# Splitting the operands of the input projection and of the memory keys and values

## The chip, the core and the metric

The kernel runs on one core of a Trainium2 chip. The metric is the device time of one execution in microseconds. Three runs of the kernel before gave 1869.04, 1870.06 and 1871.63 us, median 1870.06.

## The reference

Two layers work on 256 tokens of width 1024. Each layer does, in float32:

- RMSNorm of the residual, then one input projection (1024 rows, seven blocks of up to 256 columns). Its columns feed a state-space mixer (16 groups, 64 complex states each), six latent-attention heads, and six sparse-attention heads with a compressed, a selected and a window branch. The results are normalised and go through an output projection.
- Cross-attention: queries from the residual, keys and values from 256 normalised memory tokens (`kv = rmsnorm(mem, g_mem) @ wkv`), four heads of width 256, an output projection.
- A SwiGLU mixer, dense (width 2816) in layer 0, top-2 of 8 experts (width 3584) in layer 1.

A final RMSNorm gives the output.

## The kernel before

All weights of products with the residual or the memory are packed into chunks of 128 x 2048 float32 (1 MB). SyncE loads them in order into a ring of six slots; the slot of chunk c is loaded again with chunk c + 6 when TensorE has signalled on `weights_used` that it is done with c. A layer has 27 common chunks and then those of its SwiGLU: chunks 0 to 6 are the input projection (tiles `u`, `zA`, `zB`, `q0`, `q1`, `ck` with `cv`, `vs`), 7 to 10 the memory keys (`mk0` to `mk3`), 11 to 14 the memory values (`mv0`, `mv1`, two chunks each), 15 to 18 the output projection `wo`, 19 to 22 the queries of the cross-attention `xq`, 23 to 26 its output `xw`.

There are two kinds of product. The plain one is a float32 matmul, which stands in the trace as two matmul records. The split one takes each operand as an upper and a lower half of type fp32r and sums three matmuls, upper x upper, upper x lower and lower x upper (`split_product`, L398). For that a weight chunk is prepared: ScalarE copies it with rounding into an upper slot (`layer_chunk_upper`, L404), VectorE subtracts the upper half from the chunk in place in the ring (`layer_chunk_lower`, L411). An upper slot is free when the product of chunk c - 2 is done. Before the change chunks 0 to 14 use the plain product and 15 to 26, and all of the SwiGLU, the split one. The token side of `xq` is split by `transposes_upper` on ScalarE (L1499) and `transposes_lower` on VectorE (L1965).

TensorE's order of work is written out by hand. Its results go to PSUM tiles that rotate over five banks (`JOBS`, `ROT`): a tile's matmuls wait until the tile five places earlier was drained by ScalarE or VectorE. Every engine runs its own instruction list in order; semaphores join them.

The order in a layer, by lines of TensorE: transposes of the normalised rows (L1122), the seven projection chunks (L1132 in `features_out`, L1215 to L1243), small products of the latent and compressed attention (L1252 to L1323), then the loop over 18 heads (L1372). An iteration i of it issues the scores of head i + 3, in four iterations (2, 6, 10, 14) a memory-key chunk, in every odd one up to 15 the state input `bu` of one of eight state groups (L1355), the transposes of the probabilities of head i (L1382), the output product of head i - 1 (L1340), and in odd iterations from 3 on the output of the state group before (`state_outputs`, L1362).

A state group passes over three engines: VectorE rotates and scans it (`states`, L1892), GpSimd rotates it back with four operations (L2108 to L2116), TensorE multiplies it (L1365). VectorE also masks the scores (`masked_scores`) and, in iterations 6 and 12 and after the loop, scales the outputs of six heads (`group_outputs`). ScalarE takes the exponentials and drains the transposed probabilities.

After the loop come the memory values (`tokens_out`, L1136), between them the gate of the state-space mixer, then the split part: `wo`, `xq`, cross-attention, `xw`, SwiGLU.

GpSimd builds the rotation table of the states (`ftab`, L2081 to L2101) with the buffer of the memory keys as its scratch, and after the projection scales the transposed memory tokens into `memT`, which lies in `col` (L2105).

Of the kernel before, what the change touches and what calls it, by code (L numbers as in the profile page):

```python
# [91 lines left out]
for _i in range(4):  # L92
    _job(f"hT{_i}", "act")
# [5 lines left out]
for _n, _e in (("cqT", "act"), ("ckvT", "act"), ("hid", "dve"), ("qn0", "act"), ("qr0", "dve"), ("qn1", "act"),  # L99
# [6 lines left out]
SPLIT_FIRST = 15  # L106
# [46 lines left out]
def trunk(nc, x, mem, weights, lparams, consts, onehot, relb, fgain, out, scratch, routed, expert_out):  # L153
    with ExitStack() as ctx:
# [42 lines left out]
        kcT = sb("kcT", [P, 16])  # L197
        pcs = sb("pcs", [96, T])
# [15 lines left out]
        colr = over("colr", [P, KD, T], "col")  # L214
        xor = over("xor", [P, KD, T], "big", KD * T)
# [33 lines left out]
        memT = col  # L249
# [41 lines left out]
        s_out = sem("s_out")  # L291

# [20 lines left out]
        memT_ready = lsem("memT_ready")  # L313
# [33 lines left out]
        moe = []  # L347
        for i in range(2):
            moe.append({n: sem(f"moe{i}_{n}") for n in (
                "onehot", "gathered", "xe", "oh_t", "oh", "silu", "hid", "htr", "ht", "y", "scat", "added",  # L350
                "upper", "split", "ht_up", "xe_up", "index", "sent", "rows0", "rows1", "stored", "ye_free", "fetched",
                "merged")})
# [50 lines left out]

        def layer_chunk_upper(act, l, c):  # L404

            act.wait_ge(landed[c % RING], 16 * (LAYER_CHUNKS // RING * l + c // RING + 1))
            if c >= SPLIT_FIRST + 2:
                act.wait_ge(weights_used, l * LAYER_CHUNKS + RING + c - 1)
            act.activation(upper[:, c % 2, :], ring[:, c % RING, :], ACT.Copy).then_inc(wt_upper[l], 1)  # L409

        def layer_chunk_lower(dve, l, c):  # L411
            dve.wait_ge(wt_upper[l], c - SPLIT_FIRST + 1)
            dve.tensor_tensor(lower[:, c % RING, :], ring[:, c % RING, :], f32(upper[:, c % 2, :]), ALU.subtract).then_inc(wt_split[l], 1)  # L413
# [136 lines left out]
        def moe_pe(pe, m, used, first):  # L550


            def operands(c, count):

                pe.wait_ge(m["split"], count)
# [12 lines left out]
            def turn(i, g):  # L568
                pe.wait_ge(m["hid"], g + 1)
# [4 lines left out]
            def down(i, g, start=False, stop=False, final=False):  # L574
                up, lo = operands(3 * i + 2 if final else 3 * i + 4, 3 * g + (3 if final else 5))
                pe.wait_ge(m["ht"], g + 1)
# [8 lines left out]
            def gather_first():  # L585

                pe.wait_ge(m["onehot"], 1)
# [6 lines left out]
            def turn_rows(e, buf, loads):  # L594

                pe.wait_ge(m[f"rows{buf}"], 16 * loads)
                pe.wait_ge(m["xe"], e)
# [4 lines left out]
            def turn_onehot():  # L602
                pe.wait_ge(m["onehot"], 2)
# [4 lines left out]
            def scatter_last():  # L608
                pe.wait_ge(m["y"], NE + 1)
# [1730 lines left out]
```

## Time and profile before

| What | Value |
|---|---|
| Median of three runs | 1870.06 us |
| The profiled execution itself | 1872.84 us |
| Its span, first to last instruction | 1871.0 us |
| TensorE busy | 1738.9 us, 93% |
| VectorE busy | 1258.9 us, 67% |
| ScalarE busy | 1024.1 us, 55% |
| GpSimd busy | 189.3 us, 10% |
| Chain that ended last: TensorE, VectorE, ScalarE | 84%, 7%, 3% |
| Mean granted TensorE clock | 0.964 |

Busy time is summed over the whole span, in which stages differ. The chain follows the work back from the last instruction: a line in it had nothing slack behind it. The profiled execution took 1.84 us more than its span. The positions below are microseconds from the start of the span; layer 0 covers 26 to 539, layer 1 the rest.

### The profile page before, as it was taken

What the parts mean: (1) busy time and instruction counts of PE and PEld (TensorE: products, weight loads), DVE (VectorE), ACT (ScalarE), POOL (GpSimd) and SP (SyncE); (2) the same over time, 40 slices, a digit from 0 to 9 for tenths busy, and PEclk for the clock granted to TensorE, in tenths of its full rate; (3) what the DMA queues carried; (4) which work ended last, traced back from release to release, by engine and by line L of the source; (5) the groups of instructions that cost most, each with busy time, mean ns of one, the idle gap of its engine ahead of it and who ended that gap; (6) DMA issues with size and microseconds to landing.
All of it is one profiled execution on the core that took longest, in us unless ns stands there. A gap on an engine that the chain in (4) does not pass through costs nothing.

```text
span 1871.0 us, 23430 instructions
## 1 busy us (share of the span) xinstructions
PE 1738.9 (93%) x8104; PEld 1417.6 (76%) x8104; DVE 1258.9 (67%) x1453; ACT 1024.1 (55%) x1156; POOL 189.3 (10%) x248
## 2 busy tenths in 40 slices
PE   6989889799979899896999999999999999999995
PEld 4877477688868675775788888888888888888784
DVE  3245445545442454454799999898999988989895
ACT  2142333443421423342677777777777777777773
POOL 2614100000026141002100000000000000000200
PEclk9989999899989899897999999999999999999998
DMA  8301332755534012322999999999999999999992
GB/s 335 138 23 46 111 117 106 287 197 184 183 120 147 23 46 102 123 98 80 384 373 371 380 384 376 378 371 384 374 382 374 376 386 373 373 379 363 404 382 96
DMA packets 68404, 473.78 MB, mean 253 GB/s; under 512 B 7511, under 2 KB 9047, under 8 KB 13944
## 3 DMA queue, kind: packets, MB, share of 16 engines
q1 hardware_dynamic: 63816, 453.01, 63.7%
q0 software_dynamic: 4528, 19.98, 2.7%
q8 instruction: 36, 0.59, 0.1%
q14 instruction: 24, 0.20, 0.0%
HBM read 460.77 MB, written 12.19 MB: 253 GB/s over the span
## 4 chain that ended last, share of the span: by engine, by line
PE 84%; DVE 7%; ACT 3%; issue 2%; POOL 2%; DMA 1%; DVEq 0%; POOLq 0%; ACTq 0%; SPq 0%
PE bank L400 21%; PE bank L402 21%; PE bank L401 21%; PE bank L1132 5%; PE bank L1145 3%; ACT upper L428 1%; PE bank L571 1%; DVE xel L901 1%; POOL lp L2065 1%; PE bank L1424 1%; PE bank L1215 1%; PE bank L1243 1%; PE bank L1236 1%; DVE xor L1970 1%; DVE lp L1687 1%
## 5 line engine op out<-in xcount | busy, mean ns | idle before, releaser
L434 DVE TENSOR_TENSOR lower<-ring,upper 128x2048 fp32r<-128x2048 f32 x369 | 845.2, 2291 | 145.4 <-ACT upper L428 130.3
L428 ACT ACTIVATE upper<-ring 128x2048 fp32r<-128x2048 f32 x369 | 705.9, 1914 | 115.7 <-PE bank L402 109.6
L400 PE MATMUL bank<-upper,xeu 128*128 128x512 f32 x896 | 360.5, 402 | 5.9 <-DVE xel L901 3.4
L402 PE MATMUL bank<-upper,xel 128*128 128x512 f32 x896 | 351.1, 392 | 0.0
L401 PE MATMUL bank<-lower,xeu 128*128 128x512 f32 x896 | 350.1, 391 | 0.0
L400 PE MATMUL bank<-upper,htu 128*128 128x512 f32 x536 | 209.8, 391 | 5.5 <-DVE htl L915 3.9
L402 PE MATMUL bank<-upper,htl 128*128 128x512 f32 x536 | 208.8, 389 | 0.0
L401 PE MATMUL bank<-lower,htu 128*128 128x512 f32 x536 | 208.7, 389 | 0.0
L400 PEld LDWEIGHTS bank<-upper,xeu 128*128 128x128 f32 x896 | 168.6, 188 | 38.3 <-DVE xel L901 3.6
L402 PEld LDWEIGHTS bank<-upper,xel 128*128 128x128 f32 x896 | 168.5, 188 | 36.1
L401 PEld LDWEIGHTS bank<-lower,xeu 128*128 128x128 f32 x896 | 169.1, 189 | 31.9
L400 PEld LDWEIGHTS bank<-upper,htu 128*128 128x128 f32 x536 | 100.6, 188 | 31.3 <-issue 9.9
L402 PEld LDWEIGHTS bank<-upper,htl 128*128 128x128 f32 x536 | 100.6, 188 | 21.1
L401 PEld LDWEIGHTS bank<-lower,htu 128*128 128x128 f32 x536 | 100.6, 188 | 20.5
L413 DVE TENSOR_TENSOR lower<-ring,upper 128x2048 fp32r<-128x2048 f32 x24 | 54.8, 2291 | 80.6 <-ACT upper L409 80.6
L1132 PE MATMUL bank<-col,ring 128*128 128x256 f32 x448 | 104.4, 394 | 1.9 <-ACT col L1496 1.9
L1132 PEld LDWEIGHTS bank<-col,ring 128*128 128x128 f32 x448 | 89.0, 199 | 15.9 <-ACT col L1496 2.7
L730 ACT ACTIVATE htu<-bank 128x256 fp32r<-128x256 f32 x112 | 43.2, 386 | 99.2 <-PE bank L571 98.9
L726 ACT ACTIVATE big<-bank 128x256 f32<-128x256 f32 x112 | 43.0, 384 | 69.2 <-PE bank L402 69.2
L409 ACT ACTIVATE upper<-ring 128x2048 fp32r<-128x2048 f32 x24 | 45.6, 1908 | 57.0 <-PE bank L402 57.0
L400 PE MATMUL bank<-upper,colu 128*128 128x512 f32 x176 | 70.3, 400 | 5.4 <-DVE coll L824 5.4
L2065 POOL TENSOR_TENSOR small<-small,cst 128x2 f32<-128x2 f32 (+2 forms) x12 | 10.8, 900 | 622.8 <-DVE small L1693 614.9
(354 smaller groups left out, 2256.3 us busy)
## 6 DMA issues: line engine op xcount, KB each, us to landing
ring<-in_weights SPq DMA_DIRECT2D x423, 1024.0 KB, 6.8
routed_rows<-g POOLq DMA_DIRECT2D x1, 4096.0 KB, 27.2
lp<-in_lparams POOLq DMA_DIRECT2D x1, 3634.5 KB, 13.0
lp<-in_lparams SPq DMA_DIRECT2D x1, 3584.0 KB, 26.7
memraw<-routed_rows POOLq DMA_DIRECT2D x7, 512.0 KB, 8.4
expert_rows<-xk POOLq DMA_DIRECT2D x7, 512.0 KB, 8.7
skewed_bias<-big SPq DMA_DIRECT2D x1, 1152.0 KB, 12.3
row<-in_mem SPq DMA_DIRECT2D x1, 1024.0 KB, 4.9
```

The lines of the kernel that those rows point to most:

```text
L400: pe.matmul(to, x_up, w_up, start=start, stop=False, skip_group_check=True)
L401: pe.matmul(to, x_up, w_lo, start=False, stop=False, skip_group_check=True)
L402: return pe.matmul(to, x_lo, w_up, start=False, stop=stop, skip_group_check=True)
L409: act.activation(upper[:, c % 2, :], ring[:, c % RING, :], ACT.Copy).then_inc(wt_upper[l], 1)
L413: dve.tensor_tensor(lower[:, c % RING, :], ring[:, c % RING, :], f32(upper[:, c % 2, :]), ALU.subtract).then_inc(wt_split[l], 1)
L428: act.activation(upper[:, q % 3, :], ring[:, q % RING, :], ACT.Copy).then_inc(done, 1)
L434: dve.tensor_tensor(lower[:, q % RING, :], ring[:, q % RING, :], f32(upper[:, q % 3, :]), ALU.subtract).then_inc(done, 1)
L726: act.activation(gs[:, i % 2, 0, :], banks[i % 2][:, 0:256], ACT.Silu).then_inc(m["silu"], 1)
L730: act.activation(htu[:, i % 2, 0:256], banks[2][:, 0:256], ACT.Copy).then_inc(m["ht_up"], 1)
L1132: ins = mm(b[:, m * T:(m + 1) * T], w[:, k * 256 + m * P:k * 256 + (m + 1) * P], col[:, k, :], start=(k == 0), stop=(k == KD - 1))
L1145: ins = mm(bank(name)[:, :], src[:, 4 * part + k, t * P:(t + 1) * P], w[:, k * 512:(k + 1) * 512], start=(part == 0 and k == 0), stop=(par ...
L2065: return pool.tensor_tensor(out, a, b, op)
```

## The change

Chunks 0 to 14 use the split product too. Nothing of what is computed changes; a float32 product becomes three fp32r products.

- Weight chunks 0 to 14 are prepared by `layer_chunk_upper` and `layer_chunk_lower`. The upper halves of chunks 0 to 10 go by turns to `upper[:, 0, :]` (even, over the first 2048 columns of `attn`) and to the buffer of the memory values (odd, `coluf`); from chunk 11 on to the two slots in `attn` as before. In the loop over heads they are placed where the queries and keys in `attn` are no longer read: the upper half of chunk 7 ahead of the loop, 8 at the end of iteration 3, 9 and 10 after the drain of `mk1` and `mk2`, 11 at the end of iteration 14, 12 at the end of iteration 16. VectorE takes the lower half of chunk 7 ahead of the loop and those of 8, 9, 10, 11 and 12 in iterations 4, 8, 12, 15 and 17.
- The normalised rows are split when drained (upper half in `colr`, lower half in `coll` over the memory keys). TensorE starts `u` and `xq0` block by block as the blocks are drained.
- The window keys in `zB` are computed as tokens x columns and turned by two transposes (`kwT`).
- GpSimd's table uses `g` and the key part of `attn` as scratch; ScalarE waits for the table before it writes keys there. GpSimd scales the memory in place before `vs` is done, and then splits it with four copies and four subtractions.
- The memory is kept in HBM (one DMA out at the start) and read back (one DMA in after layer 0).
- The experts' two passes share their semaphores (counts offset by the pass); the first pass waits on the same counts as before.

```diff
+        def upper_slot(c):
+            if c < MEM_VALUES:
+                return coluf if c % 2 else upper[:, 0, :]
+            return upper[:, c % 2, :]
...
-            if c >= SPLIT_FIRST + 2:
+            if c >= 2:
                 act.wait_ge(weights_used, l * LAYER_CHUNKS + RING + c - 1)
-            act.activation(upper[:, c % 2, :], ring[:, c % RING, :], ACT.Copy).then_inc(wt_upper[l], 1)
+            act.activation(upper_slot(c), ring[:, c % RING, :], ACT.Copy).then_inc(wt_upper[l], 1)
...
+            def features_out(name, c, x_up, x_lo, stage=None):
                 up, lo = split_chunk(c)
...
+                        if stage and m == 0 and k % 2 == 0:
+                            wait_drained(pe, l, f"{stage}T{k // 2}")
...
-                drain_transposes(l, "h", C_MIX)
+                transposes_upper(l, "h", C_MIX)
+                for c in range(2):
+                    layer_chunk_upper(act, l, c)
...
+                act.wait_ge(ftab_ready[l], 1)
                 drained(A(kT[64:96, :, :], bank("ckvT")[64:96, 256:512] ...
...
+                    if i in MEMK and MEMK[i] >= 1 and MEMK[i] + 1 < XH:
+                        layer_chunk_upper(act, l, MEM_FIRST + MEMK[i] + 1)
                     wait_tile(act, l, f"pT{i}")
...
+                    if i + LEAD == NH:
+                        layer_chunk_upper(act, l, MEM_FIRST + 1)
+                    if i + LEAD == HEADS - 1:
+                        layer_chunk_upper(act, l, MEM_VALUES)
+                    if i == HEADS - 2:
+                        layer_chunk_upper(act, l, MEM_VALUES + 1)
...
+                LOWERS = {4: MEM_FIRST + 1, 8: MEM_FIRST + 2, 12: MEM_FIRST + 3, 15: MEM_VALUES, 17: MEM_VALUES + 1}
                 for i in range(LEAD):
                     masked_scores(i)
+                layer_chunk_lower(dve, l, MEM_FIRST)
                 for i in range(HEADS):
                     if i + LEAD < HEADS:
                         masked_scores(i + LEAD)
+                    if i in LOWERS:
+                        layer_chunk_lower(dve, l, LOWERS[i])
                     if i in STATES:
                         states(STATES[i])
...
+                layer_chunk_lower(dve, l, MEM_VALUES + 3)
+                layer_chunk_lower(dve, l, 15)
```

## Rows read from the trace of the kernel before

**Rows 1.** Chain that ended last, in order of time: start us, us, what.
```profile
33.17 9.56 PE bank L1132 x32
42.74 6.91 PE bank L1215 x32
49.65 3.56 PE bank L1223 x32
53.20 3.47 PE bank L1226 x16
56.67 13.81 PE bank L1132 x64
70.49 6.91 PE bank L1236 x32
```

**Rows 2.** Timeline of ScalarE, `wo` and `xq`: start, us, instruction [idle before <-releaser].
```profile
245.74 1.92 ACT L409 ACTIVATE upper<-ring 128x2048 fp32r<-128x2048 f32 x1 [3.53 <-PE bank L402]
251.18 1.92 ACT L409 ACTIVATE upper<-ring 128x2048 fp32r<-128x2048 f32 x1 [3.52 <-PE bank L402]
...
279.24 0.60 ACT L1626 ACTIVATE big<-bank 128x512 f32<-128x512 f32 x1 [3.37 <-PE bank L402]
...
285.00 0.60 ACT L1626 ACTIVATE big<-bank 128x512 f32<-128x512 f32 x1 [3.37 <-PE bank L402]
```

**Rows 3.** Timeline of VectorE in `xq`.
```profile
262.53 3.37 DVE L1970 SCALAR_TENSOR_TENSOR xor<-bank,lp,colr 128x256 fp32r<-128x256 f32 x8 [0.28 <-ACT colr L1505]
...
281.67 2.29 DVE L413 TENSOR_TENSOR lower<-ring,upper 128x2048 fp32r<-128x2048 f32 x1 [3.47 <-ACT upper L409]
```

**Rows 4.** Chain that ended last, after the projection.
```profile
84.30 0.11 PE bank L1252
```

**Rows 5.** Timeline of GpSimd: the table's end, state groups 1 and 2.
```profile
75.64 4.67 POOL L2065 TENSOR_TENSOR big<-big,xk 128x1024 f32<-128x1024 f32 x2
...
136.06 2.50 POOL L2065 TENSOR_TENSOR lp<-g,big 128x512 f32<-128x512 f32 x2 [7.10 <-DVE g L1908]
138.64 1.59 POOL L2065 TENSOR_TENSOR g<-lp 128x256 f32<-128x256 f32 x2
...
144.48 1.41 POOL L2065 TENSOR_TENSOR g<-lp 128x256 f32<-128x256 f32 x2
```

**Rows 6.** Timeline of TensorE in the loop over heads.
```profile
122.96 7.07 PE L1132 MATMUL bank<-col,ring 128*128 128x256 f32 x32
...
140.34 0.62 PE L1365 MATMUL bank<-g,cp 128*32 128x256 f32 x2 [1.55 <-POOLq L2116]
...
177.94 0.41 PE L1351 MATMUL bank<-vs,pt 128*128 128x64 f32 x2 [1.53 <-DVE lp L1687]
...
197.17 0.62 PE L1365 MATMUL bank<-g,cp 128*32 128x256 f32 x2 [2.96 <-POOLq L2116]
```

**Rows 7.** Timeline of VectorE in the loop over heads.
```profile
133.91 0.76 DVE L1687 TENSOR_TENSOR g<-lp 128x256 f32<-128x256 f32 x2
...
139.21 1.31 DVE L1687 TENSOR_TENSOR g<-lp 128x256 f32<-128x256 f32 x2
...
189.44 1.29 DVE L1687 TENSOR_TENSOR lp<-bank,big 128x512 f32<-128x512 f32 x2 [6.04 <-PE bank L1359]
```

**Rows 8.** Timeline of ScalarE, last exponential of the loop over heads.
```profile
188.82 0.50 ACT L1584 ACTIVATE attn<-attn,small 128x256 f32<-128x256 f32 x1
```

**Rows 9.** Chain that ended last: memory values of layer 0, `mk3` of layer 1.
```profile
198.22 15.63 PE bank L1145 x32
...
216.02 13.75 PE bank L1145 x32
...
695.33 7.71 PE bank L1132 x32
```

**Rows 10.** Stages by window: us, busy of PE, PEld, DVE, ACT, POOL; PEclk; DMA share, GB/s.
```profile
198.10:206.00 7.90, 7.90 (x16) 3.39 (x16) 5.15 (x4) 4.23 (x3) 0.00 (x0) 0.78 0.00 0
```

**Rows 11.** Timeline of VectorE behind the loop: the end of the mixer's norms.
```profile
220.68 0.24 DVE L1693 TENSOR_SCALAR small<-small 128x2 f32<-128x2 f32 x2
```

More of the change, by code:

```diff
@@ L98 @@
 _job("vs", "dve", 6)
-for _n, _e in (("cqT", "act"), ("ckvT", "act"), ("hid", "dve"), ("qn0", "act"), ("qr0", "dve"), ("qn1", "act"),
+for _n, _e in (("cqT", "act"), ("ckvT", "act"), ("kwT", "act"), ("hid", "dve"), ("qn0", "act"), ("qr0", "dve"), ("qn1", "act"),
                ("qr1", "dve"), ("kn0", "act"), ("kn1", "act"), ("kn2", "act"), ("vm0", "act"), ("vm1", "act"),
@@ L344, in trunk @@
         flag_ready = sem("flag_ready")
[L347 to L352, printed above, removed]
+        moe_sems = {n: sem(f"moe_{n}") for n in MOE_COUNTS}
+        moe = [ExpertPass(moe_sems, i) for i in range(2)]
         flag_again = sem("flag_again")
@@ L553, in operands @@
             def operands(c, count):
-                pe.wait_ge(m["split"], count)
+                pe.wait_ge(m["split"], m.at("split", count))
                 return upper[:, (first + c) % 3, :], lower[:, (first + c) % RING, :]
@@ L1207, in _ @@
                 transpose_rows("h")
-                wait_drained(pe, l, "hT3")
-                features_out("u", l, 0)
-                w = chunk(l, 1)
-                wait_free(pe, l, "zA")
-                for t in range(TT):
-                    for k in range(KD):
-                        ins = mm(bank("zA")[:, t * 256:(t + 1) * 256], col[:, k, t * P:(t + 1) * P], w[:, k * 256:(k + 1) * 256],
-                                 start=(k == 0), stop=(k == KD - 1))
-                finish("zA", ins)
@@ L1219, in _ @@
-                w = chunk(l, 2)
-                wait_free(pe, l, "zB")
-                for t in range(TT):
-                    for k in range(KD):
-                        mm(bank("zB")[:, t * 114:(t + 1) * 114], col[:, k, t * P:(t + 1) * P], w[:, k * 256:k * 256 + 114],
-                           start=(k == 0), stop=(k == KD - 1))
-                for k in range(KD):
-                    ins = mm(bank("zB")[:, 228:484], w[:, k * 256 + 114:k * 256 + 242], col[:, k, :],
-                             start=(k == 0), stop=(k == KD - 1))
@@ L1228, in _ @@
-                finish("zB", ins)
-                features_out("q0", l, 3)
-                features_out("q1", l, 4)
-                w = chunk(l, 5)
-                for v, name in enumerate(("ck", "cv")):
-                    wait_free(pe, l, name)
-                    for k in range(KD):
-                        ins = mm(bank(name)[:, 0:T], w[:, k * 256 + v * P:k * 256 + (v + 1) * P], col[:, k, :],
-                                 start=(k == 0), stop=(k == KD - 1))
-                    finish(name, ins)
@@ L1239, in _ @@
-                w = chunk(l, 6)
-                wait_free(pe, l, "vs")
-                for t in range(TT):
-                    for k in range(KD):
-                        ins = mm(bank("vs")[:, t * 256:(t + 1) * 256], col[:, k, t * P:(t + 1) * P], w[:, k * 256:(k + 1) * 256],
-                                 start=(k == 0), stop=(k == KD - 1))
-                finish("vs", ins)
+                features_out("u", 0, colr, coll, "h")
+                narrow_tokens_out("zA", 1, colr, coll)
+                narrow_tokens_out("zB", 2, colr, coll)
@@ L1261, in _ @@
                 finish("ckvT", ins)
+                wait_drained(pe, l, "zB")
+                wait_free(pe, l, "kwT")
+                for t in range(TT):
+                    ins = pe.transpose(bank("kwT")[:, t * P:(t + 1) * P], kwr[:, t, :], ident)
+                finish("kwT", ins)
                 wait_drained(pe, l, "ck")
@@ L1693, in mean_eps, with transposes_lower @@
                 return dve.tensor_scalar(ss[:, a:a + n], ss[:, a:a + n], 1.0 / width, EPS, ALU.mult, ALU.add)
+            def transposes_lower(stage, to, gain, n):
+                for i in range(4):
+                    dve.wait_ge(tr_upper[l], n + i + 1)
+                    for k in range(2):
+                        kk = 2 * i + k
+                        ins = dve.scalar_tensor_tensor(to[:, kk, :], bank(f"{stage}T{i}")[:, k * T:(k + 1) * T],
+                                                       cols[:, gain + kk:gain + kk + 1], f32(colr[:, kk, :]),
+                                                       ALU.mult, ALU.subtract)
+                    drained(ins)
             def norm_h(junk, l):
```

252 lines of the change are left out of this document (146 added, 106 removed).

## The prediction

> **What bounds the kernel now.** I read the page first (TensorE busy 93% and 84% of the chain that ended last), then the chain in order of time for layer 0, then the timelines of every engine over 26 to 300 us, where all changed work of a layer lies. The reader is to see three things. In the projection TensorE runs without a gap from 33.17 to 84.3 us, so what a product takes is what the stage takes [rows 1, 4]. In the loop over heads TensorE is not alone: four times it stands and waits, twice 1.55 us (one row stands for both, groups 1 and 3) and once 2.96 us for GpSimd's part of a state group, once 1.53 us for VectorE's `group_outputs(1)` [rows 6]. Any delay of VectorE or GpSimd there is paid in full. After the loop it is TensorE's work again, 15.63 and 13.75 us for the memory values [rows 9]. Both layers have this pattern; I count one and double. The SwiGLU parts are untouched but for semaphore counts that are equal in the first pass; the two new DMAs of 1 MB lie beside work that does not wait for them. Both at nothing.
>
> **What a product takes.** A plain chunk of 256-wide matmuls takes 6.91 us [rows 1]. A split chunk of the same shape is 48 matmuls; in `xq` the drains follow each other in 5.76 us (285.00 - 279.24) [rows 2]. So -1.15 us a chunk, if its halves are there. In 512-wide shape a plain pair takes 13.75 us [rows 9], a split chunk 5.44 us (251.18 - 245.74), a pair 10.88 [rows 2]: -2.87 us. Preparing a chunk costs 1.92 us on ScalarE and 2.29 us on VectorE, some 4.4 us in series with the handover [rows 2, 3].
>
> **Projection, per layer.** Gains: `zA`, `q0`, `q1`, `ck`/`cv`, `vs` five times 1.15 = 5.75; `zB` is 3.56 + 3.47 = 7.03 against 5.76, 1.27 [rows 1]. Costs: `u` may not start before chunk 0 is split. ScalarE comes to it only after draining the rows, when `u` now starts (33.17), so the start moves by about 1.9 + 2.3 = 4.1 us net of the 0.2 us of handover. `u` takes 9.56 against the warm 6.91, so it runs about 5.3 us at half clock [rows 1]; 5.3 us of that leave 25 of 48 matmuls, then 2.8 us: about 8, -1.5. Two transposes at 0.11 each [rows 4]: +0.2. After chunk 0 a slot's refill needs 4.4 us and has 5.76, slack 1.3. That slack hides the preparation, unless GpSimd holds VectorE (below); for the last chunks I add 0.3. The table, which ends at 80.3 [rows 5], ends later: its last part follows the drain of `zB`, which ends where it did (37.3 + 8 + 2 x 5.76 = 56.8, now 56.67) but is drained behind an upper half of 1.9 us, and two subtractions (4.6 us) fall into it: about 87. ScalarE now waits for it, and behind it are the drains of `ckvT`, `kwT` and `qn`; TensorE has the compressed-key product in between, the second `qn` is the first that needs a bank of these: +0.2, bounds 0 and 1.5. The memory split on GpSimd takes 16 operations of at most the 1.25 us of its 512-wide ones [rows 5], so it ends by 107; TensorE asks for it ahead of the loop, `mk0` itself starts at 122.96 and will at 119 [rows 6]: nothing, with some 8 us of cover, and a microsecond per microsecond beyond. Sum: -5.75 - 1.27 + 4.1 - 1.5 + 0.2 + 0.3 + 0.2 = -3.7. Bounds -6 (`u` at full clock) and 0 (each chunk stalls 0.5 us).
>
> **Loop over heads, per layer.** Gain 4 x 1.15 = -4.6. Costs, in order:
> - Chunk 7's subtraction ahead of the loop delays VectorE by 2.3 us; `mk0` follows at once and hides it. If not: 2.3.
> - Iterations 4 and 8: VectorE, having finished state group 1 (3), masks one head and issues the subtraction just while GpSimd works on that group, for which TensorE already waits 1.55 us. What happens if both engines read SBUF shows in a small case: two VectorE operations take 0.76 us, and 1.31 when the second rotation of GpSimd is running; GpSimd's two take 1.59 instead of 1.41 [rows 5, 7]. They take turns and do not overlap: 139.21 starts inside GpSimd's first operation, waits for its end, and GpSimd's next waits for VectorE. With a subtraction of 2.29 us GpSimd's remaining operations wait all of it: +2.25 each, 4.5. Bounds: 0 (no exclusion) and 3.4 each (VectorE's group behind it late as well).
> - Iteration 12: the subtraction stands ahead of `group_outputs(1)`, for which TensorE already waits 1.53 us: +2.25, and about 0.7 for the port: 2.9. Bounds 2.3 and 4.5.
> - Iteration 15: state group 7 waits behind chunk 11's subtraction, and that for its upper half, which ScalarE does after the last exponential (ends 189.3) [rows 8]: 189.3 + 1.9 + 2.3 = 193.5 and 0.1 for the handover, in place of 189.44 [rows 7]: +4.2. TensorE already waits 2.96 us for this group [rows 6]. Bounds 2.3 (if the product of `mk3` ends much earlier) and 5.0.
> - Iteration 17: chunk 12's subtraction comes directly behind the scan of group 7, ahead of GpSimd's first operation by a handover: +2.25. Bounds 0 and 2.3.
> - Drains held up by an upper half (1.9 us of ScalarE) in iterations 3, 6, 10, 14, 16: TensorE has the scores of a later head in between: +0.3.
>
> Sum: -4.6 + 4.5 + 2.9 + 4.2 + 2.25 + 0.3 = +9.55. The four waits become some 3.9, 3.9, 5 and 8 us long. Now the wait of 2.96 us is followed by a granted clock of 0.78 over 7.9 us, that is 3.4 us at 1.2 GHz, and `mv0` takes 15.63 in place of 13.75 us, 1.88 more; in layer 1 `mk3` takes 7.71, 0.80 more, behind the shorter wait [rows 9, 10]. After three of the new waits stands `mk1`, `mk2` or `mk3`. I charge 1.0 each, +3.0; bounds 0 and 1.9 each, and nearer the lower rows, since a drop can fall on a wait. `mv0` has its drop already.
>
> The Trainium skill, "SBUF — State Buffer", section "Who interferes with whom", says that a VectorE instruction with two SBUF inputs contends with a GpSimd instruction that reads SBUF, and that whichever starts first makes the other block fully. The rows agree (0.55 and 0.18 us longer). By this rule the loop is as above; if the two shared the port instead, the loop would be shorter by up to 7.5 us a layer, which is the first rival.
>
> **Memory values to `xq`, per layer.** `mv0` 15.63 to 10.88 + 1.9 = 12.8: -2.85. `mv1`: -2.87, but VectorE subtracts its second chunk only behind the norms of the mixer, which end at 220.9, 4.9 us after `mv1` starts [rows 9, 11]; 4.9 + 2.3 = 7.2 against the 5.44 us that its first chunk gives: 1.8 us of wait, so -1.05. GpSimd's root behind that subtraction, and chunk 15's upper half (1.9 us) ahead of the drain of `mv1`, half of it hidden: +0.9. Sum -3.0; bounds -5 and -1. `xq0` may start when the first of four drained blocks is there instead of all; the eight subtractions take 3.37 us [rows 3], three quarters of it: -2.5; bounds -2.5 and -1 (a colder start).
>
> **Sum.** Per layer -3.7 + 9.55 + 3.0 - 3.0 - 2.5 = +3.35; two layers +6.7. The profiled execution took 1872.84, so 1879.5; the median of the runs lies 2.8 lower: 1876.8.
>
> **Rivals.**
> 1. The ports do not exclude, or VectorE gets its turn where GpSimd has slack, and the clock does not drop. Then iterations 4, 8 and 17 cost nothing, 12 costs 2.3 and 15 4.2: loop +2.2, layer -7.0, time 1870.1 - 14.0 = 1856.1. For it: 51 us of TensorE-bound projection, and the waits before are short. Against: the 1.31 us row. It decides where a subtraction beside GpSimd costs its group under about 0.4 us instead of 2.25. Chance 0.24.
> 2. The waits are there but the clock stays: 1870.1 + 2 x 0.35 = 1870.8. For it: two waits of 1.55 us now have full-speed products behind them. Against: rows 9 and 10. Chance 0.16.
> 3. The projection becomes bound by its preparation: GpSimd holds VectorE in every chunk past the slack of 1.3 us, 0.7 us for six chunks, and all bounds of the loop are high: layer +3.35 + 4.2 + 3 = 10.55, time 1891.2. For it: the table's operations of up to 2.3 us [rows 5]. Against: only two subtractions meet these. Chance 0.07.
>
> **How the numbers follow.** My forecast, 1876.8, has 0.53; its own range is 1871 to 1886 from the bounds of the clock and the port. A difference of 0.2% (3.7 us) is what a measurement can tell from none. Slower than 1873.8: forecast less a small part, and rival 3: 0.57. Within: rival 2 and that part: 0.19. Faster: 0.24. The range for 8 in 10 runs from 1857 to 1888.
>
> **What would show it.** `u` starting 4 us later; chunks 1 to 6 at 5.8 us each, TensorE without gaps; waits for L2116's successor of about 3.9 us in iterations 5 and 9, of 5 us ahead of head 12's output, of 8 us at the last state output, with GpSimd's rotations stretched from 4.2 to 6.4 us beside a subtraction; a second clock drop in `mk1` to `mk3`; `mv1` with a gap of 2 us in the middle. If GpSimd's rotations keep 4.2 us beside the subtractions, rival 1 holds and the time is under 1865. If the projection shows gaps at each chunk, the slack was read wrong.

## The result: slower, by more than forecast

The kernel before took 1870.06 us (median of five runs, 1869.04 to 1875.69), the changed one 1887.31 us (1884.91 to 1891.08). The ratio is 1.0088, its 95% interval 1.0068 to 1.0107: slower by 0.7 to 1.1%, a small loss, but clear of the noise. The forecast was 1876.8 us. The sign and the mechanism came as written, the size did not: +17.3 us instead of +6.7.

| Profiled execution | before | after |
|---|---|---|
| Its time; its span | 1872.84; 1871.0 us | 1886.56; 1884.8 us |
| TensorE busy | 1738.9 us | 1715.8 us |
| VectorE, ScalarE busy | 1258.9, 1024.1 us | 1340.9, 1078.4 us |
| GpSimd busy | 189.3 us | 238.8 us |
| Mean granted TensorE clock | 0.964 | 0.946 |

TensorE is busy 23 us less (3.3 us of them ahead of layer 0, where the program is the same) and the kernel takes 14 us longer: TensorE's share of the chain that ended last fell from 84% to 76%. The profile is read below in the order of the prediction. The first view is the chain of waits of the changed kernel in the projection and behind it (start us, us, what):

```profile
29.93 1.81 ACT upper L443
31.76 2.30 DVE lower L447
34.10 0.58 PE bank L428
...
81.08 4.67 POOL big L2099 x2
85.77 1.45 ACT attn L1564
87.26 2.21 PE bank L1279 x8
```

Where the chain was TensorE alone from 33.17 us on [rows 1], it now begins with chunk 0's preparation and ends with GpSimd's table, for which ScalarE waits (L1563) before a drain that TensorE needs. Between its first product and that table TensorE has no gap but 0.76 us. The timeline of ScalarE in `xq` (start, us, instruction) has the drains 5.76 us apart as before [rows 2]:

```profile
279.77 0.60 ACT L1646 ACTIVATE big<-bank 128x512 f32<-128x512 f32 x1 [5.41 <-PE bank L430]
285.53 0.60 ACT L1646 ACTIVATE big<-bank 128x512 f32<-128x512 f32 x1 [3.36 <-PE bank L430]
```

TensorE's waits in the loop over heads and behind it, from its timeline; in brackets the idle time before the instruction and what ended it. Of [rows 6], the first two lines answer to the wait of 1.55 us, the third to that of 1.53 and the fifth to that of 2.96; the fourth is new:

```profile
136.33 1.06 PE L1366 MATMUL bank<-g,cp 128*32 128x256 f32 x2 [3.59 <-POOLq L2162]
158.66 1.06 PE L1366 MATMUL bank<-g,cp 128*32 128x256 f32 x2 [3.30 <-POOLq L2162]
180.34 0.66 PE L1352 MATMUL bank<-vs,pt 128*128 128x64 f32 x2 [4.09 <-DVE lp L1707]
198.32 0.43 PE L1352 MATMUL bank<-vs,pt 128*128 128x64 f32 x2 [1.08 <-ACT pt L1610]
206.91 1.06 PE L1366 MATMUL bank<-g,cp 128*32 128x256 f32 x2 [7.70 <-POOLq L2162]
```

GpSimd's timeline for state groups 1 and 2, and VectorE's beside group 1:

```profile
130.00 4.55 POOL L2099 TENSOR_TENSOR lp<-g,big 128x512 f32<-128x512 f32 x2 [4.80 <-DVE g L1946]
134.63 1.59 POOL L2099 TENSOR_TENSOR g<-lp 128x256 f32<-128x256 f32 x2
137.89 2.50 POOL L2099 TENSOR_TENSOR lp<-g,big 128x512 f32<-128x512 f32 x2 [1.67 <-DVE g L1946]
```

```profile
130.37 3.05 DVE L447 TENSOR_TENSOR lower<-ring,upper 128x2048 fp32r<-128x2048 f32 x1
133.35 0.28 DVE L1925 CUSTOM_DVE_ANT_0 attn<-bank,btab 128x128 f32<-128x128 f32 x1
```

GpSimd's pair of group 1 takes 4.55 us, that of group 2, with no subtraction beside it, 2.50. The subtraction takes 3.05 us where it meets GpSimd and 2.29 where it does not [rows 3]: it is issued at 130.37, waits 0.76 us for the end of GpSimd's first operation, runs, and the second operation waits for it.

Behind such a wait TensorE runs at half pace. Two matmuls of `mk1`, 3.7 and 5.7 us behind the end of the wait at 136.33; their successors start 0.22 and 0.12 us later:

```profile
140.04 0.41 PE L430 MATMUL bank<-colr,lower 128*128 128x256 f32 x1
142.07 0.28 PE L430 MATMUL bank<-colr,lower 128*128 128x256 f32 x1
```

Behind the loop, the gap in the middle of `mv1` and the wait before `wo0`:

```profile
231.25 0.50 PE L428 MATMUL bank<-upper,colr 128*128 128x512 f32 x1 [1.70 <-DVE lower L447]
242.70 0.50 PE L428 MATMUL bank<-upper,colr 128*128 128x512 f32 x1 [3.93 <-DVE xor L1720]
```

`mv0` runs from 208.75 to 221.9 us, 13.2 us in place of 15.63 [rows 9].

Last the stages by window, `mk0` to `mk1` and `mk2` to `mk3` of layer 0, with the sum over five windows from the start of the loop to the gate (us; busy of PE, PEld, DVE, ACT, POOL; PEclk is the granted clock). Before:

```profile
130.07:149.19 19.12, 17.57 (x102) 14.68 (x101) 9.80 (x29) 6.04 (x22) 8.00 (x8) 1.00 0.16 56
168.30:187.57 19.27, 17.73 (x102) 14.71 (x101) 12.87 (x34) 6.15 (x21) 8.00 (x8) 1.00 0.14 54
...
sum 88.57, PE 80.55 PEld 66.40 DVE 50.23 ACT 28.88 POOL 31.98; mean PE 16.11 PEld 13.28 DVE 10.05 ACT 5.78 POOL 6.40
```

After:

```profile
124.01:146.35 22.34, 18.75 (x118) 15.93 (x117) 12.57 (x30) 7.84 (x22) 11.25 (x10) 0.85 0.14 48
167.86:191.33 23.47, 19.36 (x118) 16.11 (x117) 15.33 (x35) 7.84 (x22) 10.20 (x8) 0.85 0.13 45
...
sum 103.26, PE 83.02 PEld 69.14 DVE 64.43 ACT 39.26 POOL 40.33; mean PE 16.60 PEld 13.83 DVE 12.89 ACT 7.85 POOL 8.07
```

This view splits the loss; what TensorE's busy time lacks of the window is waits. The loop of layer 0 grew by 14.69 us (103.26 - 88.57): 12.2 us are longer waits, and 2.5 us are longer busy time, though four products should have taken 4.6 us less. So 7.1 us are a slower pace of TensorE, put down to the clock: the three windows from `mk0` to `mk3` have 0.85, 0.92 and 0.85 instead of 1.00. In layer 1 the same windows give 101.86 against 88.41 us with TensorE busy 81.56 against 80.40: 12.3 us of waits and 5.8 us of clock.

### The profile page after: what moved, and what is told of

Read it like the earlier page. It is cut to its first block, busy times and chain, and to the rows that moved or that the text cites. A ratio compares the mean times of both kernels' runs of the same rounds, so it can differ in the third digit from the quotient of the medians.

```text
span 1884.8 us, 24338 instructions
## 1 busy us (share of the span) xinstructions
PE 1715.8 (91%) x8492; PEld 1432.9 (76%) x8492; DVE 1340.9 (71%) x1499; ACT 1078.4 (57%) x1188; POOL 238.8 (13%) x266
## 4 chain that ended last, share of the span: by engine, by line
PE 76%; DVE 9%; POOL 5%; ACT 5%; issue 3%; DMA 1%; DVEq 0%; POOLq 0%; ACTq 0%; SPq 0%
PE bank L428 23%; PE bank L430 22%; PE bank L429 22%; POOL big L2099 2%; DVE lower L447 2%; POOL lp L2099 1%; ACT upper L462 1%; PE bank L605 1%; ACT upper L443 1%; DVE xel L935 1%; POOL g L2099 1%; POOL small L2099 1%; DVE lower L468 1%; PE bank L1339 1%; PE bank L1424 1%
## 5 line engine op out<-in xcount | busy, mean ns | idle before, releaser
L468 DVE TENSOR_TENSOR lower<-ring,upper 128x2048 fp32r<-128x2048 f32 x369 | 845.2, 2291 | 144.9 <-ACT upper L462 131.0
L462 ACT ACTIVATE upper<-ring 128x2048 fp32r<-128x2048 f32 x369 | 705.9, 1914 | 114.3 <-PE bank L430 109.6
L447 DVE TENSOR_TENSOR lower<-ring,upper 128x2048 fp32r<-128x2048 f32 x44 | 104.7, 2379 | 128.2 <-ACT upper L443 128.2
L443 ACT ACTIVATE upper<-ring 128x2048 fp32r<-128x2048 f32 x44 | 84.1, 1912 | 88.9 <-PE bank L430 88.9
L430 PE MATMUL bank<-colr,lower 128*128 128x256 f32 x384 | 111.6, 291 | 0.0
L2099 POOL TENSOR_TENSOR small<-small,cst 128x2 f32<-128x2 f32 (+2 forms) x12 | 14.8, 1230 | 585.8 <-DVE small L1713 577.7
L428 PE MATMUL bank<-colr,upper 128*128 128x256 f32 x256 | 78.2, 305 | 11.8 <-DVE lower L447 11.8
L430 PE MATMUL bank<-upper,coll 128*128 128x512 f32 (+1 forms) x240 | 87.4, 364 | 0.0
```

The lines of the kernel that those rows point to most:

```text
L428: pe.matmul(to, x_up, w_up, start=start, stop=False, skip_group_check=True)
L430: return pe.matmul(to, x_lo, w_up, start=False, stop=stop, skip_group_check=True)
L443: act.activation(upper_slot(c), ring[:, c % RING, :], ACT.Copy).then_inc(wt_upper[l], 1)
L462: act.activation(upper[:, q % 3, :], ring[:, q % RING, :], ACT.Copy).then_inc(done, 1)
L468: dve.tensor_tensor(lower[:, q % RING, :], ring[:, q % RING, :], f32(upper[:, q % 3, :]), ALU.subtract).then_inc(done, 1)
L2099: return pool.tensor_tensor(out, a, b, op)
```

## The experiments

Theory A, from the prediction: a VectorE subtraction with two SBUF inputs and GpSimd's operations take turns, which lengthens waits that TensorE already had, and the clock falls behind them. Rival B: VectorE is full, and the subtraction's own time is what counts. "Before" was run beside each set, on three chips, with medians of 1872.30, 1870.02 and 1875.27 us; compare kernels of different sets by ratio. Each kernel is told by what differs from the one that its expectation names.

### Preparation moved beside the memory keys

```diff
                         m = MEMK[i]
+                        if m == 0:
+                            wait_tile(act, l, "s5")
+                        if m < 3:
+                            layer_chunk_upper(act, l, MEM_FIRST + m + 1)
                         wait_tile(act, l, f"mk{m}")
...
-                    if i in MEMK and MEMK[i] >= 1 and MEMK[i] + 1 < XH:
-                        layer_chunk_upper(act, l, MEM_FIRST + MEMK[i] + 1)
...
-                    if i + LEAD == NH:
-                        layer_chunk_upper(act, l, MEM_FIRST + 1)
...
-                LOWERS = {4: MEM_FIRST + 1, 8: MEM_FIRST + 2, 12: MEM_FIRST + 3, 15: MEM_VALUES, 17: MEM_VALUES + 1}
+                LOWERS = {2: MEM_FIRST + 1, 6: MEM_FIRST + 2, 10: MEM_FIRST + 3, 15: MEM_VALUES, 17: MEM_VALUES + 1}
```

> The changed kernel, with chunks 8, 9 and 10 prepared while TensorE works on memory-key chunks 7, 8 and 9 (ScalarE's copies and VectorE's subtractions in iterations 2, 6 and 10), not in iterations 4, 8 and 12. Theory A (a VectorE subtraction that reads two buffers of SBUF keeps GpSimd's operations waiting, and those end last for TensorE in the short iterations): GpSimd's pairs behind 130 and 152 go back from 4.55 to 2.50 us, TensorE's waits of 3.59, 3.30 and 4.09 us to about 1.5 us each, and with them two or three half-clock stretches: 7 to 9 us less in each layer, about 1871 us in all. The first state group may be held instead (2.05 us), with nobody waiting for it. The wait of 7.70 us behind chunk 11 stays. Rival B (VectorE is simply full, and the subtraction costs its 2.2 to 3.05 us wherever it stands): the waits shrink by less than half, 1880 us or more. Rival C (GpSimd and TensorE are slower because the three-pass products read more): the pairs stay at 4.55 us, 1885 us or more.

Measured: 1861.32 us (six runs), ratio 0.9935, 0.9911 to 0.9959. That is 26 us less than the changed kernel by the medians and 29 by the ratios, not 16, and faster than the kernel before. TensorE's waits are as forecast:

```profile
135.22 0.62 PE L1366 MATMUL bank<-g,cp 128*32 128x256 f32 x2 [1.55 <-POOLq L2162]
153.18 0.62 PE L1366 MATMUL bank<-g,cp 128*32 128x256 f32 x2 [1.55 <-POOLq L2162]
170.52 0.41 PE L1352 MATMUL bank<-vs,pt 128*128 128x64 f32 x2 [1.54 <-DVE lp L1707]
```

GpSimd's timeline, groups 1 and 2:

```profile
130.94 2.50 POOL L2099 TENSOR_TENSOR lp<-g,big 128x512 f32<-128x512 f32 x2 [2.80 <-DVE g L1946]
133.52 1.59 POOL L2099 TENSOR_TENSOR g<-lp 128x256 f32<-128x256 f32 x2
136.78 4.58 POOL L2099 TENSOR_TENSOR lp<-g,big 128x512 f32<-128x512 f32 x2 [1.67 <-DVE g L1946]
```

The subtraction still blocks GpSimd, now in group 2, and it costs nothing: 5.76 us of `mk1` lie before TensorE asks for that group. What I had put too low is the clock ("two or three half-clock stretches" within 7 to 9 us a layer). The windows of this kernel:

```profile
124.95:142.91 17.96, 16.41 (x118) 14.40 (x117) 12.78 (x31) 7.84 (x23) 13.23 (x11) 1.00 0.17 60
...
sum 90.01, PE 76.15 PEld 65.17 DVE 64.26 ACT 39.37 POOL 40.33; mean PE 15.23 PEld 13.03 DVE 12.85 ACT 7.87 POOL 8.07
```

The window is 4.38 us shorter than in the changed kernel, 2.04 us by the wait and 2.34 us by TensorE's busy time for the same 118 matmuls, at 1.00 instead of 0.85. Rivals B and C (1880 and 1885 us or more) are out.

### The same VectorE time with one and with two SBUF inputs

```diff
+                    if i in (4, 8):
+                        dve.wait_ge(mem_split[l], 4)
+                        dve.tensor_reduce(small[:, 440:441], memrf.bitcast(F32), AX.X, ALU.max)
```

> The kernel e1_in_mk with one more VectorE operation in iterations 4 and 8, where the subtractions of chunks 8 and 9 had stood: a maximum over one half of the memory, 128x2048, one SBUF input, its result is read by nobody. It takes VectorE about 2.2 us, like a subtraction. Theory A: GpSimd's pair stays at 2.50 us, TensorE's waits stay near 1.5 us, the time within 3 us of e1_in_mk. Rival B (VectorE's own time counts, not the port): the waits grow as in the changed kernel, 3.3 to 3.6 us, 6 to 8 us over e1_in_mk.

```diff
+                    if i in (4, 8):
+                        dve.wait_ge(mem_split[l], 4)
+                        dve.tensor_tensor(coluf if i == 4 else upper[:, 0, :], memrf.bitcast(F32), f32(colrf), ALU.subtract)
```

> The kernel e1_in_mk with one more VectorE operation in iterations 4 and 8: a subtraction of the two halves of the memory, 128x2048, two SBUF inputs, into an upper buffer that is empty there; its result is read by nobody. Theory A: GpSimd's pair beside it takes 4.55 us again, TensorE's waits there 3.3 to 3.6 us, and the clock falls behind them: 5 to 8 us over e1_in_mk and nearly as much over e2_one_read. Rival B: the same time as e2_one_read.

Measured: one input 1857.52 us (four runs, ratio 0.9908, 0.9878 to 0.9939), two inputs 1877.41 us (ten runs, 1.0017, 1.0000 to 1.0034). VectorE's timeline and GpSimd's, one input:

```profile
131.26 2.28 DVE L1983 TENSOR_REDUCE small<-memr 128x1 f32<-128x2048 f32 x1
```

```profile
130.88 2.50 POOL L2102 TENSOR_TENSOR lp<-g,big 128x512 f32<-128x512 f32 x2 [2.75 <-DVE g L1946]
133.46 1.41 POOL L2102 TENSOR_TENSOR g<-lp 128x256 f32<-128x256 f32 x2
```

Two inputs:

```profile
134.89 3.05 DVE L1983 TENSOR_TENSOR colu<-memr,colr 128x2048 fp32r<-128x2048 f32 x1
```

```profile
134.52 4.55 POOL L2102 TENSOR_TENSOR lp<-g,big 128x512 f32<-128x512 f32 x2 [3.65 <-DVE g L1946]
139.15 1.59 POOL L2102 TENSOR_TENSOR g<-lp 128x256 f32<-128x256 f32 x2
```

Both operations start within 0.4 us of GpSimd's first and keep VectorE for 2.3 us. With one input GpSimd's pair stays as it was and TensorE waits 1.36 and 1.37 us; with two the pair grows by 2.05 us and TensorE waits 3.60 us both times. So the two inputs count and not VectorE's time, and rival B is refuted: 20 us lie between two kernels in which VectorE has the same work. The two operations differ in one more thing: the maximum writes one column, the subtraction 2048. That rival is settled by a row of e1_in_mk. VectorE's first operation on group 2 has one input from PSUM (`bank`) and one from SBUF and writes 128x512; it starts 0.68 us before the end of the pair at 130.94 above, and neither is longer for it (1.29 and 2.50 us):

```profile
132.76 1.29 DVE L1707 TENSOR_TENSOR lp<-bank,big 128x512 f32<-128x512 f32 x2 [0.22 <-PE bank L1360]
```

The size surprised me again: 16 us over e1_in_mk, where I expected 5 to 8, while one input came 4 us under it, for which its waits (1.36 in place of 1.55 us) account only in part. Four operations at 2.2 us of wait each make 9 us; the windows of the four collisions are 22.80, 21.61, 21.58 and 22.84 us against 17.77 us, so each costs 3.8 to 5.1 us. The rest is busy time at a clock of 0.85 or 0.92. In layer 0 this execution also has 0.91 in the next window, behind a wait of only 1.54 us.

### Only the projection split

The memory's products are plain float32 matmuls on the memory scaled in place, chunks 7 to 14 are not prepared, and 15 and 16 are prepared where they were before:

```diff
-                        features_out(f"mk{MEMK[i]}", MEM_FIRST + MEMK[i], colr, memr)
+                        plain_features_out(f"mk{MEMK[i]}", MEM_FIRST + MEMK[i])
...
-                tokens_out("mv0", MEM_VALUES, colr, memr)
+                plain_tokens_out("mv0", MEM_VALUES)
```

> Only the projection part of the change: chunks 0 to 6 are split, the memory's chunks 7 to 14 are plain float32 products of the memory scaled in place, and chunks 15 and 16 are prepared where they were before the change. Theory A (the loss is made inside the loop over heads, by the preparation of the memory's chunks): the loop is as before the change, the projection gains about 1 us per layer up to the loop and the cross-attention queries some 3 us: 1862 us, range 1858 to 1867. Rival (the projection's own waits and the clock levels that they leave cost the loop its time): 1870 us or more. Size of the memory-value part by difference: 2.8 us per layer are missing here.

Measured: 1864.75 us (seven runs), ratio 0.9949, 0.9926 to 0.9972. The loop's waits are those of the kernel before (1.55, 1.55, 1.53, 2.96 us), up to the end of the compressed attention it gains 3.0 us per layer, and the queries 3.5 and 2.9 us. So this half of the change pays, and the loss of the whole is made in the loop. The rival is refuted as an account of the loss. Even so, with these short waits two windows of the loop in layer 0 stood at 0.92 and took 20.80 and 20.90 us, against 19.11 and 19.27 in the kernel before.

### The last iterations: chunk 11, then chunk 12

```diff
-            if c < MEM_VALUES:
+            if c <= MEM_VALUES:
                 return coluf if c % 2 else upper[:, 0, :]
...
+                        if m == 3:
+                            layer_chunk_upper(act, l, MEM_VALUES)
...
-                LOWERS = {2: MEM_FIRST + 1, 6: MEM_FIRST + 2, 10: MEM_FIRST + 3, 15: MEM_VALUES, 17: MEM_VALUES + 1}
+                LOWERS = {2: MEM_FIRST + 1, 6: MEM_FIRST + 2, 10: MEM_FIRST + 3, 14: MEM_VALUES, 17: MEM_VALUES + 1}
```

> The kernel e1_in_mk, and the upper half of chunk 11 in the buffer of the memory values, so that it need not wait for the last scores: ScalarE copies it before the drain of mk3, VectorE subtracts in iteration 14, while TensorE works on chunk 10. In e1_in_mk VectorE stood 6.69 us before that subtraction, took 2.2 us for it, and only then turned to state group 7. Theory A (TensorE's wait of 7.70 us before the last state output is made of this subtraction ahead of group 7, and of the subtraction of chunk 12 that holds GpSimd's pair): the wait falls by some 2.3 us or a little more, to 5 to 5.4 us; GpSimd's pair stays at 4.4 us; 2 to 4 us less per layer, about 1856 us. Rival B (the wait is all from chunk 12's subtraction and GpSimd): no change, 1861 us.

```diff
-                LOWERS = {2: MEM_FIRST + 1, 6: MEM_FIRST + 2, 10: MEM_FIRST + 3, 14: MEM_VALUES, 17: MEM_VALUES + 1}
+                LOWERS = {2: MEM_FIRST + 1, 6: MEM_FIRST + 2, 10: MEM_FIRST + 3, 14: MEM_VALUES}
...
+                layer_chunk_lower(dve, l, MEM_VALUES + 1)
                 layer_chunk_lower(dve, l, MEM_VALUES + 2)
```

> The kernel e5_slot11, and chunk 12's subtraction behind VectorE's last step of the state outputs (uT), not ahead of the last group of heads. Theory A: GpSimd's pair of group 7 goes back from 4.4 to 2.5 us, TensorE's last wait to the 2.96 us of the kernel before, and part of the half-clock stretch around it goes: 2 to 4 us less per layer than e5_slot11, about 1850 us. Rival: chunk 12 is then late for the second half of mv0, and TensorE waits there instead: the same time as e5_slot11.

Measured: 1851.38 us (0.9906, 0.9874 to 0.9938) and 1850.93 us (0.9906, 0.9875 to 0.9936), four runs each. The first is 10 us under e1_in_mk by the medians, but of another chip: by the ratios it is 5. The wait before the last state output, first of chunk 11's kernel, then of chunk 12's:

```profile
190.05 1.06 PE L1366 MATMUL bank<-g,cp 128*32 128x256 f32 x2 [3.47 <-POOLq L2162]
```

```profile
186.93 1.06 PE L1366 MATMUL bank<-g,cp 128*32 128x256 f32 x2 [1.53 <-POOLq L2163]
```

Chunk 11 was worth more of the wait than I expected (7.70 to 3.47, expected 5 to 5.4 us), because VectorE had not only done this subtraction ahead of group 7 but had also stood before it for its upper half. Chunk 12 was worth the rest; `mv0` did not become late. The runs do not tell the two kernels apart (spreads of 6 and 9 us); the traces do. Up to the last state output the loop is 4.3 us shorter in layer 0 and 1.5 us in layer 1. Of this only what lies behind the drain of `mk3` belongs to the edit, 1.9 and 1.5 us (11.35 us became 9.41 and 9.82), which is the shorter wait; the other 2.3 us of layer 0 come before it.

### The table, the start, the gate, the blocks

```diff
-                    y = kTf[:, 512:512 + 8 * m].rearrange(...)
+                    y = (ptf[:, 0:8 * m] if m >= 64 else kTf[:, 512:512 + 8 * m]).rearrange(...)
...
-                act.wait_ge(ftab_ready[l], 1)
                 drained(A(kT[64:96, :, :], ...
```

(ScalarE waits for the table ahead of the loop instead.)

> The kernel e6_late12, and GpSimd's table has its large scratch in pt and not in the keys' buffer, so that ScalarE need not wait for the table before it drains the keys' rotary part. Theory A (my reading of the changed kernel: this wait costs TensorE 1.0 us and the queries' products behind it about 1.5 us): 1.0 to 1.5 us less per layer, about 1847 us. Rival: another drain ends last there and nothing changes.

Measured: 1841.88 us (four runs), 0.9848, 0.9818 to 0.9878. TensorE's wait of 1.02 us at L1279 is gone, and from `cqT` to the last `vm` both layers take 1.29 us less (14.16 against 15.45 us), as expected. That accounts for 2.6 of the 9 us between the medians; the rest is not explained by this edit. The spreads overlap (1838.97 to 1845.88 against 1843.83 to 1853.14), and the two profiled executions stand the other way round, 1845.88 us here and 1843.83 for e6_late12.

```diff
+                    act.wait_ge(weights_used, RING + LAYER_CHUNKS)
+                layer_chunk_upper(act, l, 0)
                 scale_rows(1)
...
+                layer_chunk_lower(dve, l, 0)
                 transposes_lower("h", coll, C_MIX, 0)
-                layer_chunk_lower(dve, l, 0)
```

> The kernel e7_table, and chunk 0 prepared before the rows' halves: ScalarE copies it before it scales the rows, VectorE subtracts while TensorE turns the rows, and then lowers the rows' blocks. In the changed kernel TensorE waits 5.08 us before its first product for this subtraction, and the eight products behind run in part at half clock (8.0 us for u). Theory A: the wait shrinks to under 1.5 us, u ends 3.5 to 5 us earlier: about 7 to 10 us in all less than e7_table, about 1839 us. Rival (in layer 0 the chunk lands too late, or the rows' blocks end last anyway): less than 3 us in all.

Measured: 1834.86 us (four runs), 0.9814, 0.9785 to 0.9842, 7 us less than the kernel before it. `u` ends 4.0 and 4.5 us earlier in the two layers. The copy and the subtraction are still made; what had cost this time was their place behind the rows' halves, in both lists. In the changed kernel the copy was the one that ended last: VectorE stood 0.87 us before the subtraction until ScalarE, done with its drains, had made it:

```profile
31.76 2.29 DVE L447 TENSOR_TENSOR lower<-ring,upper 128x2048 fp32r<-128x2048 f32 x1 [0.87 <-ACT upper L443]
```

So the run does not say what moving the subtraction alone would bring.

```diff
+                layer_chunk_upper(act, l, MEM_VALUES + 3)
                 wait_tile(act, l, "gl")
                 drained(A(pt[:, 0, :], bank("gl")[:, :], ACT.Tanh, scale=0.5))
-                layer_chunk_upper(act, l, MEM_VALUES + 3)
+                layer_chunk_upper(act, l, 15)
...
-                layer_chunk_upper(act, l, 15)
                 memory_values(1)
...
+                layer_chunk_lower(dve, l, MEM_VALUES + 3)
                 wait_tile(dve, l, "yr")
...
-                layer_chunk_lower(dve, l, MEM_VALUES + 3)
                 layer_chunk_lower(dve, l, 15)
```

> The kernel e8_start, and chunks 14 and 15 prepared earlier: ScalarE copies chunk 14 before the gate's tanh and 15 before it scales the rows, VectorE subtracts chunk 14 before the gate. In e8_start TensorE waits 1.70 us for chunk 14 and 3.92 us (2.93 us in the kernel before the change) for the lower halves of the output projection's rows, which stand behind the subtraction of chunk 15. Theory A: the first wait goes and the second falls back to 2.9 us: 2 to 3 us less per layer, about 1830 us. Rival: the gate comes later by the subtraction and the rows with it, and nothing is won: 1835 us.

Measured: 1831.87 us (five runs), 0.9779, 0.9752 to 0.9805. The wait of 1.70 us is gone, the other fell from 3.92 to 2.98 us; by the traces, from the drain of `mk3` to the scaled rows behind `wo`, 2.4 and 2.7 us less per layer.

```diff
+                            if turned and t == 0 and k % 2 == 0:
+                                wait_drained(pe, l, f"{turned}T{2 * part + k // 2}")
...
-                wait_drained(pe, l, "yT3")
-                tokens_out("wo0", 15, colr, xor)
+                tokens_out("wo0", 15, colr, xor, "y")
```

> The kernel e9_gate, and the output projection wo0 started block by block as the rows' blocks are drained, as the change does for u and xq0. Expected: the wait of 2.9 us before its first product shrinks to under 1.5 us, 1.5 to 2.5 us less per layer, about 1826 us. Rival: the blocks come at the pace of VectorE (0.8 us a block of two), TensorE waits as long in small pieces and keeps half clock longer: the same time.

Measured: 1825.67 us (five runs, 1822.71 to 1826.40), 0.9738, 0.9716 to 0.9761. This is the best version: 2.6% under the kernel before, 3.5% under the changed one by the ratios (1.0088 / 0.9738 = 1.036). Its gain was larger than expected, 3.9 and 3.7 us per layer from the first drained block of the rows to the scaled rows behind `wo`; the wait fell to 0.72 us:

```profile
212.12 0.47 PE L429 MATMUL bank<-upper,colr 128*128 128x512 f32 x1 [0.72 <-DVE xor L1723]
```

```diff
+                wait_drained(pe, l, "xT3")
                 for i in range(XH):
-                    features_out(f"xq{i}", 19 + i, colr, xor, "x" if i == 0 else None)
+                    features_out(f"xq{i}", 19 + i, colr, xor)
```

> The kernel e9_gate with one part of the change undone: xq0 waits for all four blocks again before its first product. It measures the term that I put at 2.5 us per layer (bounds 0.5 to 3): about 1835 us, 5 us over e9_gate. Rival (TensorE then idles in small pieces instead): within 1 us of e9_gate.

Measured: 1841.11 us (four runs), 0.9828, 0.9799 to 0.9857, 9.2 us over e9_gate. The wait that comes back is only 2.08 us:

```profile
244.21 0.39 PE L429 MATMUL bank<-colr,upper 128*128 128x256 f32 x1 [2.08 <-DVE xor L1723]
```

but from the scaled rows to the end of `xq0` both layers take 14.19 us instead of 10.56 and 10.54: 3.6 us per layer, 7.3 of the 9.2 us.

## Why the prediction was right in sign and short in size

The measured 1887.31 us lies outside the forecast's own range (1871 to 1886) and 0.7 us inside the range for 8 in 10 (1857 to 1888), whose width came from the rivals, none of which describes what happened: that it still held is luck. Errors also cancelled, as the table shows: the clock, the projection and `wo` came out dearer than forecast, the waits and `xq` cheaper.

Per layer, from the drains that stand at the same point of both kernels (layer 0 and 1 where they differ):

| Step | Forecast | Measured |
|---|---|---|
| Projection, up to the last `vm` | -3.7 | -1.9, -2.0 |
| Compressed attention, to the loop | 0 | +0.9, +1.3 |
| Loop, waits | +13.9 | +12.2, +12.3 |
| Loop, held-up drains | +0.3 | within the waits |
| Loop, products and clock | -4.6 + 3.0 | +2.5, +1.2 |
| Memory values | -3.0 | -2.8, -2.9 |
| `wo` | 0 | +2.1, +0.5 |
| `xq` | -2.5 | -3.6, -3.0 |
| Cross-attention, up to SwiGLU's norm | 0 | -0.8, 0.0 |
| Sum | +3.35 | +8.6, +7.5 |

- Projection. `u` took 8.0 us as forecast and the products behind it 5.76; at `cqT` 3.4 and 3.5 us were won. The failed term is the wait for the table, put at 0.2 us with bounds 0 and 1.5: e7_table measures 1.29 us. The reader was the second `qn` (the wait stands behind the first eight records of L1279) and the table's end came at 85.7 us, not 87, so the path was read rightly and the price was not worked out: ScalarE's drain behind the table (L1564) takes 1.44 us and ends at 87.21, while TensorE is there at 86.24. That `u` started 4.0 us later, counted from the scaled rows, is as forecast.
- Compressed attention. The +0.9 and +1.3 us are TensorE's pace on the same 44 matmuls, not work of the change: over the thirteen profiles this stretch took 9.5 to 13.4 us (last section).
- Iterations 4, 8: forecast +2.25 each, measured +2.04 and +1.75. Iteration 12: +2.9, measured +2.56. Iterations 15 and 17: +6.45 together, measured 4.74 at the state output and 1.08 just before it. Mechanism and size hold, and e2_one_read and e3_two_reads show the cause in iterations 4 and 8: the two SBUF inputs beside GpSimd. GpSimd's rotations of group 1 took 6.22 us in all (130.00 to 136.22), forecast 6.4. The Trainium skill, "SBUF — State Buffer", section "Who interferes with whom", is borne out in both halves that these runs test: two SBUF inputs block (4.55 us for 2.50), one does not (2.50 us).
- The clock is the term that was mis-sized: "I charge 1.0 each, +3.0". It took 7.1 us in layer 0 and 5.8 in layer 1. I had priced it by two rows of the kernel before, 1.88 and 0.80 us, and then taken less than their mean because "a drop can fall on a wait". The nearest row was the one of 1.88 us, behind 2.96 us of wait: all new waits were longer. Nor does the drop fall on the wait: the slow pace stands over the products that follow, for 5 us in `mk1` (136.33 to about 141.4). After a wait of 3.3 us or more the window around it ran at 0.85 or 0.92, in all six windows of the changed kernel and in all four collisions of e3_two_reads, and took 1.5 to 2.8 us more. With waits of 1.3 to 1.6 us 47 of 68 such windows in the other profiles stood at 1.00 and 21 at 0.91 or 0.92, at a cost of 1.5 to 1.8 us; none stood at 0.85. So behind the longer waits the drop came ten times in ten and was sometimes deeper, and a short wait does not rule it out. (The prices are against the same matmuls at 1.00, for the changed kernel those of e1_in_mk.) The window of the last wait had 0.72 in place of 0.97, with TensorE 1.0 us busier for the same work.
- Memory values: `mv0` 13.2 us (forecast 12.8), the gap in `mv1` 1.70 (forecast 1.8).
- `wo` had no term. Chunk 15's subtraction stands ahead of the rows' lower halves, and TensorE's wait there grew from 2.93 to 3.93 us in both layers; e9_gate gives that back. What else differs, +1.1 and -0.5 us, no run explains.
- `xq`: 3.6 us by e11_xq_whole, not 2.5. I priced the wait only (2.08 us in e11_xq_whole) and nothing for the slower start behind it. In the changed kernel the gain was 3.6 and 3.0 us.
- The rows of the table make 16.1 us, the span grew by 13.8. The other -2.3 us are -3.07 ahead of layer 0, where the program is the same (last section), -0.94 in the SwiGLU of layer 0 and +1.75 in that of layer 1, in which no product changed.

Rival 1 was wrong on the exclusion, rival 2 on the clock. Rival 3 (1891.2 us) came nearer to the measured time than the forecast did, for a wrong reason: the projection was not bound by its preparation. The rival that was missing is the one that came, in which the clock costs about half as much as the waits (7.1 and 5.8 us beside 12.2 and 12.3).

## What to carry to other kernels

Ask, in a kernel like this, of each added VectorE operation with two SBUF inputs whose GpSimd operation it will meet, and who waits for that; put it where the engine behind GpSimd has a long product of its own. Here the same three subtractions cost 13.3 us in layer 0 in short iterations, clock included, and nothing beside the long products (from the end of `mk0` to that of `mk3` 67.3 us against 54.0). Charge a wait on TensorE that grows from 1.5 to 3.5 us with the 2 us and with 1.5 to 2.8 us more for the clock behind it, less what the short wait sometimes cost already. And measure the halves of a change apart before giving it up: by the ratios the projection's half gained 0.5% (e4_proj_only) and the memory's half, as placed, cost 1.4%; placed as in e6_late12 the whole stood at 0.9906, 0.4% better than the projection alone, which is little beside the intervals. Moving eight preparations, one scratch buffer and one wait turned +0.9% into -2.6%.

## What the runs showed of the hardware

- VectorE beside GpSimd: one SBUF input or two decides, not the time on the engine. A reduction of 128x2048 from SBUF left GpSimd's pair at 2.50 us, a subtraction of the same length made it 4.55. A second input from PSUM does not count (e1_in_mk, 1.29 and 2.50 us).
- The same instructions take very different time in different executions. The stretch from the last `vm` to `pcs` has the same 44 matmuls in every kernel. By window, of e5_slot11 and of e1_in_mk (layer 1):

```profile
96.74:106.22 9.48, 5.30 (x44) 4.68 (x44) 2.40 (x9) 5.51 (x9) 6.62 (x7) 0.96 0.00 0
```

```profile
604.33:617.75 13.42, 9.22 (x44) 8.38 (x44) 2.40 (x9) 5.72 (x9) 6.61 (x7) 0.59 0.00 0
```

  3.9 us lie between them, at 0.96 and 0.59. The bias products ahead of layer 0 (L1200, in the changed kernel L1226) took 8.05 us in the kernel before and 4.98 in the changed one, with no change there. Here the granted clock does not tell the two apart: the slower has 1.00. By window of 11 to 24 us, before and after:

```profile
11.00:24.00 13.00, 11.62 (x28) 7.12 (x28) 3.34 (x7) 3.03 (x5) 0.00 (x0) 1.00 1.01 421
```

```profile
11.00:24.00 13.00, 8.36 (x28) 5.55 (x28) 5.80 (x11) 3.19 (x5) 1.27 (x2) 0.79 1.01 416
```

  All thirteen profiles are of one of these two kinds: in seven the same 28 matmuls keep TensorE busy for 11.62 us at 1.00 and layer 0 begins at 27.3 to 27.6 us, in six for 8.3 to 8.4 us at 0.79 to 0.84 and it begins at 24.1 to 24.3. So a stage of few microseconds in one trace cannot be credited to an edit unless the busy time of the same matmuls is compared too, and the granted clock beside it is not always enough. What sets which of the two a run gets stays open.
